# Mixture-of-experts output of a streaming encoder layer: gated expert rows added to sums in memory by accumulating scatters

## What is computed

```
g_prob = softmax(h @ w_rg + b_rg);  p_top, g_top = top_k(g_prob, 1)
v_top, i_top = top_k(e_logits in group g_top, 2)
gates = softmax(v_top) * p_top
for each expert e, for its tokens:  out = (silu(xb @ w_gate[e]) * (xb @ w_up[e])) @ w_down[e]
y = sum over a token's two experts of gate * out
x = x + y;   result = RMSNorm(x) * g_final
```

## Time and profile before

| | |
|---|---|
| median of three runs | 1176.58 us |
| the profiled execution: its time | 1175.42 us |
| its span, first to last instruction | 1173.6 us |
| TensorE busy | 1035.8 us (88%) |
| VectorE, ScalarE, GpSimd busy | 379.9, 280.5, 235.2 us |
| moved by DMA | 267.57 MB, of it 201 MB weights of experts |
| mean granted TensorE clock | 0.942 |

### The profile page before, as it was taken

One profiled execution on the slowest core, in us unless ns is written; L12 is line 12 of the kernel. 1 busy time (PEld: TensorE's weight loads), 2 busy tenths in 40 slices (PEclk: granted clock), 3 DMA queues, 4 the chain that ended last, 5 costly groups with the idle time before them and its releaser, 6 DMA issues. The chain is left out here.

```text
span 1173.6 us, 15244 instructions
## 1 busy us (share of the span) xinstructions
PE 1035.8 (88%) x6331; PEld 719.1 (61%) x6331; DVE 379.9 (32%) x704; ACT 280.5 (24%) x445; POOL 235.2 (20%) x131
## 2 busy tenths in 40 slices
PE   2987999999998998999999889978888787778896
PEld 2976787776988888999999733333333333333332
DVE  6067323333367617422222521211111111110117
ACT  5233533436245525222211400000000000000003
POOL 3322111210422117544422001111100111100100
PEclk7988999998999979999999889999999888998898
DMA  8236011110311112334338699999999999999993
GB/s 201 73 76 215 20 54 37 51 40 19 91 54 37 45 49 68 92 101 140 90 112 347 229 356 427 427 426 426 425 429 425 429 427 427 428 427 425 426 410 144
DMA packets 109472, 267.57 MB, mean 228 GB/s; under 512 B 22478, under 2 KB 89326, under 8 KB 96195
## 3 DMA queue, kind: packets, MB, share of 16 engines
q1 hardware_dynamic: 104706, 258.06, 57.5%
q0 software_dynamic: 4704, 8.64, 1.9%
HBM read 256.12 MB, written 18.17 MB: 234 GB/s over the span
## 5 line engine op out<-in xcount | busy, mean ns | idle before, releaser
L1366 PE MATMUL proj<-we,xsT 128*64 128x512 f32 x512 | 252.2, 650 | 68.3 <-DMA we<-in_w_exp_up 62.0
L1368 PE MATMUL proj<-we,xsT 128*64 128x512 f32 x512 | 252.7, 651 | 0.0
L862 POOL TENSOR_TENSOR wlo<-raw,whi 128x1024 fp32r<-128x1024 f32 x70 | 162.5, 2321 | 422.4 <-PE proj L1000 409.8
L1366 PEld LDWEIGHTS proj<-we,xsT 128*64 128x64 f32 x512 | 73.5, 149 | 212.9 <-issue 197.6
L1000 PE MATMUL proj<-hT_hi,whi 128*128 128x272 f32 x704 | 151.7, 297 | 10.7 <-DVE hT_lo L265 8.2
L1000 PE MATMUL proj<-hT_lo,whi 128*128 128x272 f32 x704 | 149.3, 294 | 0.0
L1000 PE MATMUL proj<-hT_hi,wlo 128*128 128x272 f32 x704 | 149.0, 294 | 0.0
L1524 ACT CAST whi<-raw 128x1024 fp32r<-128x1024 f32 x70 | 69.8, 999 | 223.5 <-PE proj L1000 213.6
L2259 DVE TENSOR_TENSOR hg<-hg,proj 64x512 f32<-64x512 f32 x32 | 22.1, 690 | 312.3 <-ACT hg L1820 296.0
L1000 PEld LDWEIGHTS proj<-hT_hi,whi 128*128 128x128 f32 x704 | 113.3, 193 | 15.1 <-DVE hT_lo L265 8.3
L1820 ACT ACTIVATE hg<-proj 64x512 f32<-64x512 f32 x30 | 17.7, 591 | 424.6 <-PE proj L1368 424.6
(11 more groups left out here) (329 smaller groups left out, 1430.0 us busy)
## 6 DMA issues: line engine op xcount, KB each, us to landing
we<-in_w_exp_gate SPq DMA_DIRECT2D x31, 2048.0 KB, 32.1
we<-in_w_exp_up SPq DMA_DIRECT2D x31, 2048.0 KB, 36.6
we<-in_w_exp_down SPq DMA_DIRECT2D x31, 2048.0 KB, 38.9
raw<-in_w_in SPq DMA_DIRECT2D x43, 512.0 KB, 3.8
expert_out<-S_smp SPq DMA_DIRECT2D x1, 4352.0 KB, 14.9
x_rows<-in_x_prompt SPq DMA_DIRECT2D x8, 512.0 KB, 4.7
raw<-in_w_branch_b SPq DMA_DIRECT2D x8, 512.0 KB, 3.9
raw<-in_w_out SPq DMA_DIRECT2D x8, 512.0 KB, 4.0
```

The lines of the kernel that those rows point to most:

```text
L862: nc.gpsimd.tensor_tensor(lo[:, 0:c], raw[n % NRAW][:, 0:c], hi[:, 0:c].bitcast(F32), ALU.subtract).then_inc(w_split, 1)
L1366: pe.matmul(proj[0:SLOTS, s, 0, :], xsT[:, k, cols], wg[:, k * FF:(k + 1) * FF], start=(k == 0), stop=(k == KD - 1))
L1368: mm = pe.matmul(proj[64:64 + SLOTS, s, 0, :], xsT[:, k, cols], wu[:, k * FF:(k + 1) * FF], start=(k == 0), stop=(k == KD - 1))
```

## The change

- `expert_out`, its zeros and the clearing of their source go. In their place is `row_sums`, 2 x 544 rows of 2 KB, one sum of 4 KB for each token. SP stores x into it: tiles 0 and 1 between the stores of h2, tiles 2 to 4 behind the load of expert 1's down weights.
- The gates of all slots are turned into lane order (`slot_gate`): 40 small matmuls more before the first gather is turned; the 20 for the second choice, the 10 of L1356 and the two `pick` tables go.
- `rows_out` multiplies by `slot_gate` where it copied, and writes `sidx` first. `S1` is 2 x token + half.
- A scatter adds to its rows in memory (`compute_op=ALU.add`). Since a token's two experts may meet in one row, GpSimd waits before each scatter until the one before has landed.
- Expert 30 is scattered too, when the other 30 have landed. SP loads its down weights ahead of the gate and up weights of expert 31, and TensorE takes down(30) ahead of up(31).
- When scatter 30 has landed, SP loads the sums into x, 4 KB for each token. Expert 31 alone goes by `last_rows`, with a table `pick` of ones and its gates applied by ScalarE in the copy of `yo`. `add_gated`, `second_rows` and their diagonals go; a dummy root on ScalarE stands before the end's squares.

```diff
-    ys = nc.dram_tensor("expert_out", (4 * TOK, FF), F32, kind="Internal").ap()
+    sums = nc.dram_tensor("row_sums", (2 * TOK, FF), F32, kind="Internal").ap()
...
-                sp.wait_ge(consts_set, 1)
-                sp.dma_start(ys.rearrange("(n p) d -> p n d", p=P), zeros).then_inc(ys_zeroed, 16)
...
+        for i in range(2):
+            store_normed(i)
+            store_plain(i)
+        for i in range(2, NT):
+            store_normed(i)
         sp.wait_ge(x2_turned, NT)
         load_expert(1, 2, 1)
+        for i in range(2, NT):
+            store_plain(i)
...
+        sp.wait_ge(down_done, NE - 4)
+        load_expert((NE - 2) % NSETS, 2, NE - 2)
         sp.wait_ge(up_done, NE - 3)
         for part in range(2):
             load_expert((NE - 1) % NSETS, part, NE - 1, slice(0, 2048))
...
-        sp.wait_ge(down_done, NE - 4)
-        load_expert((NE - 2) % NSETS, 2, NE - 2)
...
+        sp.wait_ge(sums_set, 16 * NT)
+        sp.wait_ge(ys_stored[0], 16 * PAIRS)
         for i in range(NT):
-            sp.dma_start(zc[i][0:ROWS[i], :, :].rearrange("p c d -> p (c d)"), pair_rows[i * P:i * P + ROWS[i], :])\
-                .then_inc(rows_loaded[i], 16)
+            sp.dma_start(X[0:ROWS[i], i, :], sum_rows[i * P:i * P + ROWS[i], :]).then_inc(rows_loaded[i], 16)
...
+            pool.indirect_dma_start(out=sums[:, :], out_offset=bass.IndirectOffsetOnAxis(ap=sidx[s][:, 0:1], axis=0),
+                                    in_=yo[:, s, :], in_offset=None, bounds_check=2 * TOK - 1, oob_is_err=False,
+                                    compute_op=ALU.add).then_inc(done, 16)
...
         def put(it, u):
+            if u > 0 or not (isinstance(it, int) and it == 0):
+                pool.wait_ge(ys_stored[(u - 1) % 2], it * (16 * NSETS) + 16 * ((u + 1) // 2))
             pool.wait_ge(yo_ready, it * (2 * NSETS) + u + 1)
...
+        pool.sem_inc(others_stored, 1)
+        pool.wait_ge(yo_ready, NE - 1)
+        scatter(0, ys_stored[0])
...
-            v.tensor_copy(yo[:, s, :], proj[:, s, 1, :])
+            v.tensor_scalar(yo[:, s, :], proj[:, s, 1, :], slot_gate[:, cols], None, ALU.mult).then_inc(yo_ready, 1)
...
+        dve.wait_ge(others_stored, 1)
+        v.tensor_scalar(sidx[0][:, :], S1[:, NE - 2:NE - 1], 1.0, None, ALU.mult)
+        dve.wait_ge(down_done, NE - 1)
+        v.tensor_scalar(yo[:, 0, :], proj[:, 0, 1, :], slot_gate[:, NE - 2:NE - 1], None, ALU.mult).then_inc(yo_ready, 1)
```

More of the change, by code:

```diff
@@ L328, in _build @@
     gate = R("gate", [P, 2, NT])
-    last_gates = R("last_gates", [P, NT, 2])
+    slot_gate = R("slot_gate", [P, NBLK])
     RING = R.at
@@ L666, in _build @@
     U_ = Region(RT)
-    pick = [U_(f"pick{s}", [P, TOK]) for s in range(2)]
+    pick = U_("pick", [P, TOK])
     xsb2 = U_("xsb2", [P, D])
@@ L921, in pair @@
         def pair(it, m):
-            if not first_pair(it, m):
+            if first_pair(it, m):
+                pool.wait_ge(sums_set, 16 * NT)
+            elif m:
                 put(it, 2 * m - 1)
+            else:
+                put(it - 1, 2 * NSETS - 1)
             put(it, 2 * m)
@@ L1451, in _, with last_rows @@
         n0, n1 = we_loaded[(NE - 2) % NSETS], we_loaded[(NE - 1) % NSETS]
[L1453 removed]
+        def last_rows(i):
             r = ROWS[i]
@@ L1458, in last_rows @@
                 rows_ = slice(64 * half, 64 * half + 64)
[L1459 to L1470, removed]
+                mm = pe.matmul(out[0:r, half, :], pick[rows_, i * P:i * P + r], yo[rows_, 1, :], start=True, stop=True)
+            mm.then_inc(picked, 1)
         def up_half(k):
@@ L1493, in _ @@
         down(0, w0[2], down_done)
+        up(1, slice(SLOTS, P), w1[0], w1[1], up_done, up_half)
         pe.wait_ge(act_done[1], PAIRS)
         turn_hidden(1, hT2_done)
-        pe.wait_ge(last_y, 1)
-        last_rows(0, 0, True, False)
         pe.wait_ge(hT2_copied[1], PAIRS)
         down(1, w1[2], down_done, down_half)
[L1500 to L1508, removed]
+        pe.wait_ge(pick_ready, 1)
+        pe.wait_ge(yo_ready, NE - 1)
+        pe.wait_ge(last_y, 1)
+        for i in range(4):
+            last_rows(i)
         pe.wait_ge(comb_done, 1)
-        last_rows(0, 4, True, False)
-        last_rows(1, 4, False, True)
+        last_rows(4)
     @block.scalar
@@ L2245, in _ @@
         v.tensor_copy(meta[0:1, :], bef[0:1, :]).then_inc(meta_ready, 1)
-        run(v.tensor_scalar(S1[:, :], G1[:, :], 4.0, con("half"), ALU.mult, ALU.add))
-        dve.wait_ge(second_done, 1)
-        run(v.scalar_tensor_tensor(S1[:, :], choice, 2.0, S1[:, :], ALU.mult, ALU.add))
+        run(v.tensor_scalar(S1[:, :], G1[:, :], 2.0, con("half"), ALU.mult, ALU.add))
+        dve.wait_ge(slot_gates_done, 1)
+        v.tensor_copy(slot_gate[:, :], bank[:, 3, 0:NBLK]).then_inc(slot_gates_copied, 1)
+        dve.wait_ge(slot_gates_copied, 1)
         dve.wait_ge(meta_ready, 1)
-        dve.wait_ge(late_loaded, 32)
-        for s in range(2):
-            dve.wait_ge(gate_rows_done, s + 1)
-            row_ = proj[:, s, :, :].rearrange("p a b -> p (a b)")[:, 0:TOK]
-            last = v.scalar_tensor_tensor(pick[s][:, :], numbers, G1[:, NE - 2 + s:NE - 1 + s], row_, ALU.is_equal, ALU.mult)
-        last.then_inc(picks_ready, 1)
         def gated(s, done):
```

115 lines of the change are left out of this document (43 added, 72 removed).

## The result

| | before | after |
|---|---|---|
| median (runs) | 1175.25 us (15) | 1180.39 us (15) |
| lowest to highest | 1173.36 to 1178.83 | 1177.63 to 1184.93 |
| profiled execution's span | 1173.6 us | 1179.3 us |
| mean granted TensorE clock | 0.942 | 0.931 |

A forecast was written before the change was run, and what follows sets the result against it. Engines were taken to bound up to 687.36 us, with TensorE setting the pace, transfers to 1123.03, engines the rest. -6.8 + 1.0 + 9.5 - 4.8 = -1.1 against the 1176.58 median gave 1175.5 us; range 1163 to 1196.

The forecast's parts named there:

- The zeros: Near 100 us: without the zero-fill transfer the weight tile behind it is in time, TensorE's gap mostly goes: -6.8 us.
- The router: Before up(0): added gate matmuls cost 0; stores of x tiles 2 to 4 delay the first gather: +1.0 us.
- The scatters: Experts' stretch: reading each added row's old value counts the bytes of 29 scatters a second time: +9.5 us.
- The 11.3 us: Scatter cost in the experts' stretch if memory-SBUF transfers were held to some 358 GB/s; unused because rows show 426.
- The free read: Rival for the adding scatters: reading the old row fits into the engine's write side; total 1166.0 us; chance 0.27.
- two passes: Rival for the adding scatters: two or more further passes, 1185.0 us with two, 1194.5 with three; chance 0.21.
- The waits: GpSimd's waits between scatters: landing takes 12 us, issues are 14.6 apart, so 0; costs from 14.7 us on.
- The end: After up(30): first sum starts 2.6 us later, VectorE's work to the last store shrinks by 7.4: -4.8 us.
- two spells at the lower clock: TensorE after up(30): slower steps in down(30), +1.7 us, and again in down(31), which ends at 1152.4 against 1149.8.
- Two signs: Signs of being right: up(0) some 6 us earlier; wait for expert 30's up weights ending near 1127.
- The remark that the page's bytes read would rise: Profile page: bytes read from memory up by the scatters' 4.3 MB less 2.2 of smaller loads at the end.

The follow-up runs named there:

- the half rows: Kernel before with scatters carrying only each row's first 1 KB, plain and adding: experts' stretch 429.5 and 435.6 us, one execution each of 1171.12 and 1174.99 us.
- the old order: Changed kernel with up(31) ahead of down(30) on TensorE again, SP's and VectorE's order to match: 1179.76 us (7 runs), ratio 1.0057.

## Why the prediction was wrong

**The zeros, -6.8: right.** -6.4 at the first gather, and moving the zeros alone gave 7.0 there. These are pairs of single executions, and executions with the same work ahead of the gather lie up to 5.6 us apart there; the gap of 5.26 us that is gone is the firmer sign.

**The router, +1.0: this step failed.** It measured +5.1. The step reads: "of its four us to landing it loses at most these 2.8 and at least nothing. I take +1.0, since it moves only 0.28 MB itself". The argument let the gather share the engines by its size, and counted only tiles 2 to 4. In fact it got so little beside a full SP queue that it landed when that queue was drained, and everything in front, tiles 0 and 1 included, had made the queue longer. The earlier trace rows held the warning: a gather of 0.28 MB among the weights lands after 11.9 us, though its bytes are 0.65 us of the engines. The sound step was the one that the prediction itself used for scatters: where the engines are full, bytes push others back. 2.2 MB at 426 GB/s are 5.2 us, whichever transfer is pushed; with all five stores later the sum of the gather's time and the stretch is conserved to 0.2 us, with three to 1.1. The Trainium skill (DMA: Bandwidth & Descriptors, Queues, rings and completion order) says that an engine takes turns between the queues that have work, a packet at a time. By it the gather should take turns with SP's queue; if the turns moved equal bytes, it would be through after 0.56 MB, 1.3 us at 426 GB/s (an estimate). It landed after 9.1 us, so this trace does not bear out even turns in bytes; no run here separates the packets of the two queues.

**The scatters, +9.5: right in mechanism, low in size.** It measured +11.3 in the change, +11.6 for the adding alone. The adding costs 1.2 passes, not one. The Trainium skill (Collectives: The Full Stack, Stop ④ — SDMA + CCE: where bytes move and the add happens) describes adding on the way as "read-read-write with the add free in between", of collectives. That no third pass appears agrees, with 11.6 us where two further passes would be 19. The extra fifth is not explained; the half rows suggest that plain scatters have it too. The 11.3 us that the prediction worked out and set aside is the measured size, but the limit behind it is not seen: with the adding the counted bytes still moved at 418 GB/s. The free read (0.27) and two passes (0.21), which together were held likelier than the forecast, are both excluded.

**The waits, 0: right.** 11.1 us to landing against 14.7; the adding alone costs as much without them.

**The end, -4.8: right within its means.** -5.3 here. The forecast had two spells at the lower clock, the profiled execution has one; in the versions with all stores later and with three later it is two, and up(30) to the first sum is then 31.9 and 31.8 us (1130.19 to 1162.06, 1137.10 to 1168.86), for 31.4 forecast. In size this is partly luck: 12.7 us from the first sum to the last store's issue where 12.0 was forecast, and one spell less in front. The order of the last two experts, as the old order shows, made no difference that the medians resolve.

**The sum.** The router's term was 4.1 us too small and the scatters' 1.8. With the first put right the sum reads +3.0, no longer a gain; with both, +4.8. The profiled spans differ by 5.7: the rest is the 0.9 of the clock in up(0). Two signs that the prediction named show the same: up(0) starts 1.2 us earlier (677.34 for 678.50) and not some 6, and the wait for expert 30's up weights ends at 1133.98 and not near 1127. The remark that the page's bytes read would rise by 4.3 - 2.2 MB was wrong as well: they fell by 2.2 (253.89 for 256.12). The reading of old values is not counted: the adding alone leaves this number at 256.12.

## What to carry to other kernels

Where transfers bound a later stage, take it that every byte issued just ahead of it or in it costs nearly its full time, even if it is placed behind work that waits anyway: here it surfaced in the next small transfer or in the weights. For the adding, put 1.2 times the scatter's bytes on top of the plain scatter, and look for its cost in the rate of the others, not in the count of bytes. A prefill that stalls a stage is best moved to a place where the queue has slack, before anything is built to get rid of it: one line gave 0.7%, and the rebuilding lost 0.5%.

## What was not expected of the hardware

- Adding scatters take GpSimd 1.57 us each to issue for 1.00, whether the rows are 2 KB or 1 KB; GpSimd's queue has more packets for the same rows (6624 for 4704 in the adding alone, 6624 for 3744 with rows of 1 KB), and the bytes of the old rows are in none of the page's sums.
- A gather of 0.28 MB through GpSimd's queue lands with the last of what SP had queued before it: 9.1 us after its issue with the stores of x ahead. Its turn starts 9.2 us after its issue with them, 4.5 without.
- The page's rate fell with the adding (427 to 418) while the share of busy engines stayed at 1.01, so neither alone tells whether transfers got dearer.
